# A hybrid decoder block on one core: small fp32 matmuls packed into parts of the array, gate units opened early, and splits moved in three queues

## The chip, the cores and the metric

The kernel runs on one core of one Trainium2 chip. The metric is the device time of one execution in microseconds; of several runs the median is given. The kernel drives the engines directly: TensorE (PE, its weight loads PEld), VectorE (DVE), ScalarE (ACT), GpSimd (POOL) and SyncE (SP, which issues most loads) each run their own instruction list in order, and wait for one another by semaphores alone.

## The reference, cut to what matters

```python
h = rms_norm(x, norm_mix_pre)                      # x: 512 tokens x 2048
proj = h @ w_in + b_in                             # q, f, i, g | qk, v, o, ig, fg | gate_a, gate_b
# HGRN2: 8 heads of 128, chunks of 64 tokens
q = silu(q) * 128 ** -0.5;  f = lb + (1 - lb) * sigmoid(f);  k = 1 - f
b = cumsum(log f) in a chunk;  q_dec = q * exp(b);  k_inv = k * exp(-b);  k_end = k * exp(b_last - b)
attn = tril(q_dec @ k_inv.T)                       # 64 x 64 for each head and chunk
o = attn @ v + q_dec @ S;   S = exp(b_last) * S + k_end.T @ v
y_a = head_rms_norm(o) * silu(g)
# mLSTM: 4 heads, same chunkwise form with a matrix memory -> y_b
merged = sigmoid(gate_a) * (y_a @ w_up_a) + sigmoid(gate_b) * (y_b @ w_up_b)
x = x + rms_norm(merged @ w_out, norm_mix_post)    # "x1 rows"
h = rms_norm(x, norm_ffn_pre)
out = x + rms_norm((gelu(dwconv(h @ w_gate)) * (h @ w_up)) @ w_down, norm_ffn_post)   # 5632 hidden
```

## The kernel before, in words

All data is fp32. The big products are made from two fp32r parts each: a high part, rounded by ScalarE (`split_hi`), and the rest, by VectorE (`split_lo`). A product is hi x hi + hi x lo + lo x hi. Weights of the mixer come in units of 1 MB, two units in flight (`RING`), each with its own slot s = 0 or 1 of `raw`, `w_hi` and `w_lo`. TensorE's `cm_unit` does a unit as 16 matmuls of 128x512 with `w_hi` and `h_hi`, 16 with `w_hi` and `h_lo`, 16 with `w_lo` and `h_hi`, into bank 6 or 7; ScalarE evacuates it and counts `cm_evac`. A unit's high split waits until the unit two before it is done.

The units run in this order: I, F, Q, GA (merge gates of branch a), G, QK, V, GB (gates of b), O, then the lifting and the output projection. Each engine has the order written out by hand. The recurrences are woven into the gate units: a round of HGRN2 handles 128 tokens (two chunks) beside four GA units, a round of mLSTM 128 tokens beside four GB units, four rounds each.

A round of HGRN2 on TensorE, before: 8 transposes of k_end into `hT_` (banks 0, 1); 8 score matmuls of 128x128 for both chunks at once into `hA_` (banks 2, 3); unit 0; 16 state updates that use half the rows each (L753 for the first chunk, L755 for the second); 8 matmuls of masked scores `hg_at` with v, 128x128, into `hO_` (banks 4, 5); unit 1; 16 matmuls of q_dec with the states `sa` and `sb_`, each on half of the output partitions (L767, L769); unit 2; 8 transposes of the normalised outputs; unit 3. ScalarE copies the two diagonal 64x64 blocks of each head's scores out of PSUM into `hg_at`, whose rest GpSimd has set to zero once, and GpSimd masks the upper triangle (`affine_select`). VectorE updates the states, norms the outputs and makes decays and the next round's operands (`hg_prep_b`, `hg_prep`); ScalarE does the exponentials (`hg_prep`).

The entry to the feed-forward stage: the output projection's last two column blocks are done in halves (`OUT_HALVES`, k = 0 to 3, four units each; `un_out(4, q)` and `un_out(5, q)` are the splits of k = 2 and 3). For each 128 tokens n, `mix_ms`, `x1_rows` and `x1_norm` (VectorE), `x1_square` (ScalarE) and a power on GpSimd make the residual rows and their norm. The feed-forward products run as a 2x2 block scheme with seven products (M1 to M7): operands are sums or differences of blocks. The rows are summed (`diff4`, `diff3`, `sum1`, ...), turned by TensorE (`turn_pieces(r)`, 14 of them; L917), copied as high parts (`pieces_hi`), less their high part (`less_hi`, L926), and copied as rests (`pieces_rest`); `TURN_AFTER` and `need` say which rest has to be copied before which turn or product. The weight side is `weight_sum` (VectorE), `hi` (ScalarE) and `lo` (VectorE) for each position of the sequence; `times_h` multiplies (L960 for the high part, L964 for the rest).

## Time and profile before

| | |
|---|---|
| time, median of 3 runs | 2825.56 us (2824.33 to 2825.88) |
| the profiled execution | 2820.7 us |
| its span | 2819.1 us |
| TensorE busy | 2778.4 us (99%) |
| VectorE, ScalarE, GpSimd busy | 1669.9, 1230.6, 353.5 us |
| mean granted TensorE clock | 0.998 of full speed |

Times in the profile are microseconds from the span's start. A row of the timeline merges like instructions that follow each other; a bracket gives the idle time of the engine before it and who ended it. Matmuls overlap in the pipeline, so the step from one start to the next tells the cost of one, not its duration. An fp32 matmul (not fp32r) has two records.

### The profile page before, as it was taken

The numbers are of one execution on the slowest core, as the hardware profiler recorded it, in microseconds if no ns is written. First come the engines' busy times: TensorE is split into PE (matmuls) and PEld (weight loads), VectorE is DVE, ScalarE is ACT, GpSimd is POOL, SyncE is SP. The second block draws the span as 40 slices with busy tenths as digits, with TensorE's granted clock in tenths as the row PEclk, the third lists the DMA queues.
The fourth block names the chain that finished last, engine by engine and source line by source line (L and its number), as shares of the span: only waits on it lengthen the run. The fifth ranks groups of instructions, "written<-read, shape, count | busy, mean of one in ns | idle before, by whom it ended". The sixth has DMA issues, their size and how long they took to land.

```text
span 2819.1 us, 37731 instructions
## 1 busy us (share of the span) xinstructions
PE 2778.4 (99%) x13843; PEld 2345.9 (83%) x13843; DVE 1669.9 (59%) x1863; ACT 1230.6 (44%) x1469; POOL 353.5 (13%) x417
## 2 busy tenths in 40 slices
PE   8999999999999999999989999999999999999998
PEld 6888888888888888888867888888888888888887
DVE  5232334344333323442568788888878878878788
ACT  4243444332222222222465555555555555555554
POOL 1000001000000000000000122222222222222213
PEclk9999999999999999999999999999999999999999
DMA  4333333332233334444643788888888888788876
GB/s 174 90 89 104 97 101 99 99 108 94 90 94 91 97 105 138 140 142 141 215 136 120 184 175 162 181 177 161 175 180 164 169 185 164 165 189 165 161 179 239
DMA packets 451444, 404.46 MB, mean 143 GB/s; under 512 B 13074, under 2 KB 357270, under 8 KB 448552
## 3 DMA queue, kind: packets, MB, share of 16 engines
q1 hardware_dynamic: 397672, 294.69, 34.5%
q0 software_dynamic: 49088, 100.33, 21.5%
q10 hardware_dynamic: 4608, 8.39, 0.8%
q8 instruction: 52, 0.85, 0.1%
q14 instruction: 24, 0.20, 0.0%
HBM read 302.69 MB, written 100.66 MB: 143 GB/s over the span
## 4 chain that ended last, share of the span: by engine, by line
PE 96%; DVE 2%; issue 1%; ACT 1%; POOL 0%; DMA 0%; DVEq 0%; SPq 0%; POOLq 0%; ACTq 0%
PE ps L960 19%; PE ps L615 18%; PE ps L964 10%; PE ps L618 9%; PE ps L872 6%; PE ps L997 5%; PE ps L998 5%; PE ps L999 5%; PE ps L639 4%; PE ps L641 4%; PE ps L640 4%; PE ps L677 1%; PE ps L717 0%; PE ps L1063 0%; PE ps L1059 0%
## 5 line engine op out<-in xcount | busy, mean ns | idle before, releaser
L1707 DVE TENSOR_TENSOR w_lo<-raw,w_hi 128x2048 fp32r<-128x2048 f32 x127 | 291.1, 2292 | 494.2 <-ACT w_hi L1104 494.0
L1663 POOL DMA_DIRECT2D down_sums<-arena x304 | 262.8, 972 | 904.6 <-ACT arena L1419 880.3
L1104 ACT CAST w_hi<-raw 128x2048 fp32r<-128x2048 f32 x127 | 242.2, 1907 | 237.7 <-PE ps L641 175.4
L2117 DVE TENSOR_TENSOR sum_ring<-quads 128x1024 f32<-128x1024 f32 x166 | 203.4, 1225 | 171.1 <-PE ps L964 137.4
L1375 ACT CAST op_ring<-sum_ring 128x1024 fp32r<-128x1024 f32 x166 | 175.0, 1054 | 271.2 <-DVE sum_ring L2117 271.2
L615 PE MATMUL ps<-h_hi,w_hi 128*128 128x512 f32 x1152 | 276.4, 392 | 1.1 <-ACT w_hi L1104 1.1
L618 PE MATMUL ps<-h_hi,w_lo 128*128 128x512 f32 x1152 | 272.8, 389 | 0.0
L615 PE MATMUL ps<-h_lo,w_hi 128*128 128x512 f32 x1152 | 272.8, 389 | 0.0
L960 PE MATMUL ps<-hl,op_ring 128*128 128x512 f32 x1064 | 267.5, 394 | 3.6 <-ACT op_ring L1375 2.5
L615 PEld LDWEIGHTS ps<-h_lo,w_hi 128*128 128x128 f32 x1152 | 216.2, 188 | 44.9
L618 PEld LDWEIGHTS ps<-h_hi,w_lo 128*128 128x128 f32 x1152 | 216.2, 188 | 44.9
L615 PEld LDWEIGHTS ps<-h_hi,w_hi 128*128 128x128 f32 x1152 | 214.1, 188 | 46.3 <-ACT w_hi L1104 1.5
L960 PEld LDWEIGHTS ps<-hl,op_ring 128*128 128x128 f32 x1064 | 194.3, 190 | 40.4 <-issue 2.9
L2131 DVE TENSOR_TENSOR op_ring<-sum_ring,op_ring 128x1024 fp32r<-128x1024 f32 x166 | 202.1, 1217 | 8.7 <-ACT op_ring L1375 8.7
L1419 ACT COPY arena<-ps 128x512 f32<-128x512 f32 x320 | 178.3, 582 | 53.7 <-PE ps L999 42.7
L960 PE MATMUL ps<-h,op_ring 128*128 128x512 f32 x792 | 199.4, 394 | 1.9 <-ACT h L1355 1.3
L997 PE MATMUL ps<-op_ring,act_hi 128*128 128x512 f32 x480 | 187.6, 391 | 0.1
L998 PE MATMUL ps<-op_ring,act_hi 128*128 128x512 f32 x480 | 187.5, 391 | 0.0
L999 PE MATMUL ps<-op_ring,act_lo 128*128 128x512 f32 x480 | 186.7, 389 | 0.0
L960 PEld LDWEIGHTS ps<-h,op_ring 128*128 128x128 f32 x792 | 145.1, 190 | 30.2 <-ACT h L1355 2.2
L2131 DVE TENSOR_TENSOR op_ring<-quads,op_ring 128x1024 fp32r<-128x1024 f32 x129 | 157.0, 1217 | 7.6 <-ACT op_ring L1375 7.6
L964 PEld LDWEIGHTS ps<-hl,op_ring 128*128 128x128 f32 x1064 | 145.2, 190 | 10.4
(355 smaller groups left out, 4627.2 us busy)
## 6 DMA issues: line engine op xcount, KB each, us to landing
raw<-in_w_in SPq DMA_DIRECT2D x88, 1024.0 KB, 5.3
down_sums<-arena POOLq DMA_DIRECT2D x320, 256.0 KB, 6.6
quads<-in_ffn_w_gate SPq DMA_DIRECT2D x88, 512.0 KB, 4.8
quads<-in_ffn_w_up SPq DMA_DIRECT2D x88, 512.0 KB, 4.7
quads<-in_ffn_w_down SPq DMA_DIRECT2D x88, 512.0 KB, 7.6
raw<-in_w_out SPq DMA_DIRECT2D x24, 1024.0 KB, 5.0
merge_gates<-arena ACTq DMA_DIRECT2D x32, 256.0 KB, 2.0
raw<-in_w_up_a SPq DMA_DIRECT2D x8, 1024.0 KB, 5.1
```

The source lines that it names most:

```text
L615: pe.matmul(ps[:, 6 + s, :], w[0][:, j, :], k[:, j, :], start=(k is k_hi and j == 0), stop=False)
L618: last = pe.matmul(ps[:, 6 + s, :], w[1][:, j, :], k_hi[:, j, :], start=False, stop=(j == KT - 1))
L960: pe.matmul(ps[:, bank, :], w[0][:, j, :], h[:, j, :, :].rearrange("p r t -> p (r t)"), start=(j == 0 and q not in (M7, M6)), stop=False, ...
L964: mm = pe.matmul(ps[:, bank, 0:TH], w[1][:, j, :], h[:, j, 0, :], start=False, stop=(j == HALF - 1), skip_group_check=True)
L997: pe.matmul(ps[:, n, :], act_hi[:, f + j, tok], w[0][:, j, :], start=(j == 0), stop=False)
L998: pe.matmul(ps[:, n, :], act_hi[:, f + j, tok], w[1][:, j, :], start=False, stop=False)
L999: mm = pe.matmul(ps[:, n, :], act_lo[:, f + j, tok], w[0][:, j, :], start=False, stop=(j == 1))
L1104: act.copy(w_hi[:, s, :], raw[:, s, :]).then_inc(hi_ready, 1)
L1663: pool.dma_start(dst, src, accum_op=ALU.add).then_inc(acc_added[s], 16)
L1707: dve.tensor_tensor(w_lo[:, s, :], raw[:, s, :], f32(w_hi[:, s, :]), ALU.subtract).then_inc(lo_ready, 1)
L2117: dve.tensor_tensor(op_sum[slot_of(i, pos)], quads[:, a, :], quads[:, b, :], ALU.subtract if q in (M7, M6) else ALU.add).then_inc(ff_sum, 1)
L2131: dve.tensor_tensor(op_lo[slot], src, f32(op_hi[slot]), ALU.subtract).then_inc(ff_lo, 1)
```

## The change

- **Packing.** `hg_blocks` holds the scores as 128 x 8 x 64: rows are the key tokens of both chunks, columns the 64 query tokens of the same chunk, with nothing off the diagonal. The scores are 16 matmuls (each head and chunk) with 64 columns, on the half of the output partitions that belongs to the chunk. Scores times v are 16 matmuls of 64 rows and 64 output partitions: rows by chunk, output partitions by whether the head is even or odd, bank by chunk. q_dec times state goes to the same places (`by_state`); the first chunk's part now follows directly behind scores times v, the second's comes after unit 1. ScalarE's two copies of scores are one, GpSimd's mask is two smaller ones and its zeroing is gone; the outputs' last copy is two.
- **Unit 0 of each round opens early** (`unit_opens`, `unit_goes_on`): its first 16 products stand ahead of transposes and scores, in both recurrences.
- **Queues.** ScalarE: the split of Q1 ahead of the first exponentials; in a round, the outputs' copy and squares ahead of the split of unit 3. VectorE: the outputs' norm ahead of the split and of the next round's scans. At the entry to the feed-forward stage: splits ahead of squares and of x1 rows; `x1_norm` cut into `x1_ms` and `x1_scale`; `hi(0, 1)`, `hi(0, 5)` and the copy of M1 ahead of pieces and squares; the weight sums at other places. The sum for position (0, 1) has its own room (`early_sum`), and the wait for the slot moves from VectorE to ScalarE.

```diff
--- before
+++ after
@@ -191,6 +191,8 @@
+        hg_blocks = hg_at[:, 0:HG_H * CHUNK].rearrange("p (h c) -> p h c", h=HG_H)
+        CHUNK_ROWS = (slice(0, CHUNK), slice(CHUNK, P))
@@ -247,6 +249,7 @@
+        early_sum = ar(88.5, Q)
@@ -407,6 +410,13 @@
+        def ahead(i, pos):
+            return isinstance(i, int) and (i, pos) == (0, 1)
+        def sum_of(i, pos):
+            return early_sum if ahead(i, pos) else op_sum[slot_of(i, pos)]
@@ -618,6 +628,24 @@
+            def unit_opens(u, n, s):
+                pe.wait_ge(cm_evac, n + 1)
+                w = w_hi[:, s, :].rearrange("p (j n) -> p j n", j=KT)
+                split_ready(u, 0)
+                for j in range(KT):
+                    pe.matmul(ps[:, 6 + s, :], w[:, j, :], h_hi[:, j, :], start=(j == 0), stop=False)
+            def unit_goes_on(u, n, s):
+                w = [t[:, s, :].rearrange("p (j n) -> p j n", j=KT) for t in (w_hi, w_lo)]
+                for j in range(KT):
+                    pe.matmul(ps[:, 6 + s, :], w[0][:, j, :], h_lo[:, j, :], start=False, stop=False)
+                split_ready(u, 1)
+                for j in range(KT):
+                    last = pe.matmul(ps[:, 6 + s, :], w[1][:, j, :], h_hi[:, j, :], start=False, stop=(j == KT - 1))
+                last.then_inc(unit_done, 1)
@@ -734,43 +762,54 @@
-            at_, ket, sa, sb_, on = map(heads, (hg_at, hg_ket, hg_sa, hg_sb, hg_on))
+            ket, sa, sb_, on = map(heads, (hg_ket, hg_sa, hg_sb, hg_on))
+            at_ = hg_blocks
...
+                unit_opens(U_GA + 4 * i, N_GA + 4 * i, 0)
...
-                    mm = pe.matmul(hA_[:, h, :], ki[:, h, :], qd[:, h, :], start=True, stop=True)
+                    for c, rows in enumerate(CHUNK_ROWS):
+                        mm = pe.matmul(hA_[rows, h, 0:CHUNK], ki[:, h, rows], qd[:, h, rows], start=True, stop=True)
...
-                unit(0)
+                unit_goes_on(U_GA + 4 * i, N_GA + 4 * i, 0)
...
-                pe.wait_ge(hg_scores_copied, 2 * i + 2)
+                pe.wait_ge(hg_scores_copied, i + 1)
...
-                    m1 = pe.matmul(hA_[:, h, :], ket[CHUNK:P, h, :], v_hg[CHUNK:P, i:i + 1, h * P:(h + 1) * P],
-                                   start=True, stop=True)
+                    pe.matmul(hA_[:, h, :], ket[CHUNK:P, h, :], v_hg[CHUNK:P, i:i + 1, h * P:(h + 1) * P],
+                              start=True, stop=True)
...
-                pe.wait_ge(hg_scores_masked, i + 1)
+                pe.wait_ge(hg_scores_masked, 2 * i + 2)
...
-                for h in range(HG_H):
-                    pe.matmul(hO_[:, h, :], at_[:, h, :], v_hg[:, ds(i, 1), h * P:(h + 1) * P],
-                              start=(h % 4 == 0), stop=False, skip_group_check=True)
+                for pair in range(HG_H // 2):
+                    for odd, out in enumerate(CHUNK_ROWS):
+                        h = 2 * pair + odd
+                        for c, rows in enumerate(CHUNK_ROWS):
+                            pe.matmul(hO_[out, 4 * c + pair, :], at_[rows, h, :], v_hg[rows, i:i + 1, h * P:(h + 1) * P],
+                                      start=(pair == 0), stop=False, skip_group_check=True)
+                def by_state(c, state):
+                    for pair in range(HG_H // 2):
+                        for odd, out in enumerate(CHUNK_ROWS):
+                            h = 2 * pair + odd
+                            mm = pe.matmul(hO_[out, 4 * c + pair, :], qd[:, h, CHUNK_ROWS[c]], state[:, h, :], start=False,
+                                           stop=True, skip_group_check=True)
+                    return mm
+                by_state(0, sa).then_inc(hg_update1, 1)
...
-                for h in range(HG_H):
-                    m0 = pe.matmul(hO_[0:CHUNK, h, :], qd[:, h, 0:CHUNK], sa[:, h, :], start=False, stop=False,
-                                   skip_group_check=True)
-                    m1 = pe.matmul(hO_[CHUNK:P, h, :], qd[:, h, CHUNK:P], sb_[:, h, :], start=False, stop=True,
-                                   skip_group_check=True)
-                m0.then_inc(hg_update1, 1)
-                m1.then_inc(hg_out_done, 1)
+                by_state(1, sb_).then_inc(hg_out_done, 1)
@@ -802,8 +841,6 @@
-            pe.wait_ge(tok_evac, 4 + 16)
@@ -811,6 +848,9 @@
+                unit_opens(U_GB + 4 * i, N_GB + 4 * i, 0)
+                if i == 0:
+                    pe.wait_ge(tok_evac, 4 + 16)
@@ -824,7 +864,7 @@
-                unit(0)
+                unit_goes_on(U_GB + 4 * i, N_GB + 4 * i, 0)
@@ -1187,33 +1227,44 @@
+            un_q, to_q = units_of(U_Q, 2), into(q_all, ACT.Silu, 0)
+            split_hi(*un_q(0, 1))
...
-            columns(U_Q, NU_Q, into(q_all, ACT.Silu, 0))
+            act.wait_ge(unit_done, U_Q + 1 + RING)
+            to_q(0, ps[:, 6, :], 0)
+            split_hi(*un_q(0, 2))
+            act.wait_ge(unit_done, U_Q + 1 + 1 + RING)
+            to_q(1, ps[:, 7, :], 1)
+            with act.Fori(1, NU_Q // 2) as i:
+                for s in range(2):
+                    split_hi(*un_q(i, s + 1))
+                    act.wait_ge(unit_done, U_Q + 2 * i + s + 1 + RING)
+                    to_q(2 * i + s, ps[:, 6 + s, :], s)
...
-                act.wait_ge(mem_zero, 2)
...
-                for a in (0, CHUNK):
-                    act.copy(heads(hg_at)[a:a + CHUNK, :, a:a + CHUNK], hA_[a:a + CHUNK, :, a:a + CHUNK]).then_inc(hg_scores_copied, 1)
+                act.copy(hg_blocks, hA_[:, :, 0:CHUNK]).then_inc(hg_scores_copied, 1)
...
-                split_hi(*un_ga(i, 3))
...
+                split_hi(*un_ga(i, 3))
...
-                act.copy(q_all[:, :, ds(i * P, P)], hT_).then_inc(hg_out_kept, 1)
+                act.copy(q_all[:, :, ds(i * P, CHUNK)], hT_[:, 0:4, :].rearrange("p g (e t) -> p (g e) t", e=2))
+                act.copy(q_all[:, :, ds(i * P + CHUNK, CHUNK)],
+                         hT_[:, 4:8, :].rearrange("p g (e t) -> p (g e) t", e=2)).then_inc(hg_out_kept, 1)
@@ -1315,6 +1366,8 @@
+                if k == 2 and s == 0:
+                    act.wait_ge(sq_done, 1 + TT + 2)
@@ -1371,7 +1424,9 @@
-                    src = op_sum[slot]
+                    if ahead(i, pos):
+                        slot_free(act, i, pos)
+                    src = sum_of(i, pos)
@@ -1450,10 +1505,10 @@
+            split_hi(*un_out(4, 2))
...
-            split_hi(*un_out(4, 2))
+            split_hi(*un_out(4, 3))
...
-            split_hi(*un_out(4, 3))
@@ -1469,9 +1524,9 @@
+            hi(0, 1)
...
-            hi(0, 1)
@@ -1491,9 +1546,9 @@
-            pieces_rest(10)
...
+            pieces_rest(10)
@@ -1591,14 +1646,13 @@
-            pool.wait_ge(tok_evac, 4 + 8)
-            pool.memset(hg_at, 0.0).then_inc(mem_zero, 1)
...
-                pool.wait_ge(hg_scores_copied, 2 * i + 2)
-                pool.affine_select(out=heads(hg_at), in_=heads(hg_at), compare_op=ALU.is_ge, fill=0.0, base=0,
-                                   pattern=[[0, HG_H], [1, P]], channel_multiplier=-1).then_inc(hg_scores_masked, 1)
+                pool.wait_ge(hg_scores_copied, i + 1)
+                for rows in CHUNK_ROWS:
+                    pool.affine_select(out=hg_blocks[rows, :, :], in_=hg_blocks[rows, :, :], compare_op=ALU.is_ge, fill=0.0,
+                                       base=0, pattern=[[0, HG_H], [1, CHUNK]],
+                                       channel_multiplier=-1).then_inc(hg_scores_masked, 1)
@@ -1878,16 +1932,16 @@
-                split_lo(*un_ga(i, 3))
...
-                if not last:
-                    hg_prep_b(i + 1)
+                split_lo(*un_ga(i, 3))
...
+                if not last:
+                    hg_prep_b(i + 1)
@@ -2100,9 +2154,15 @@
+            def x1_ms(n):
+                row_ms(TT + n, ss2[:, n:n + 1], 4 + n)
+            def x1_scale(n):
+                row_scale(TT + n, x1[:, n, :], g_pre2, x_rows[:, n, :], 4 + n)
...
-                row_ms(TT + n, ss2[:, n:n + 1], 4 + n)
-                row_scale(TT + n, x1[:, n, :], g_pre2, x_rows[:, n, :], 4 + n)
+                x1_ms(n)
+                x1_scale(n)
@@ -2113,8 +2173,9 @@
-                slot_free(dve, i, pos)
-                dve.tensor_tensor(op_sum[slot_of(i, pos)], quads[:, a, :], quads[:, b, :],
+                if not ahead(i, pos):
+                    slot_free(dve, i, pos)
+                dve.tensor_tensor(sum_of(i, pos), quads[:, a, :], quads[:, b, :],
@@ -2126,7 +2187,7 @@
-                    src = op_sum[slot]
+                    src = sum_of(i, pos)
@@ -2252,14 +2313,14 @@
+            split_lo(*un_out(4, 1))
...
-            split_lo(*un_out(4, 1))
+            split_lo(*un_out(4, 2))
...
-            split_lo(*un_out(4, 2))
+            split_lo(*un_out(4, 3))
...
-            split_lo(*un_out(4, 3))
+            split_lo(*un_out(4, 4))
...
-            split_lo(*un_out(4, 4))
@@ -2269,32 +2330,34 @@
+            weight_sum(0, 1)
...
-            weight_sum(0, 1)
+            lo(0, 1)
+            x1_ms(2)
...
-            lo(0, 1)
-            x1_norm(2)
-            x1_norm(3)
-            weight_sum(0, 2)
+            x1_scale(2)
+            x1_ms(3)
+            x1_scale(3)
...
-            lo(0, 2)
+            weight_sum(0, 2)
...
+            lo(0, 2)
...
-            lo(0, 4)
...
+            lo(0, 4)
```

## Rows read from the trace of the kernel before

**Rows 1.** Busy time, share and instructions of each engine (the page).
```profile
PE 2778.4 (99%) x13843; PEld 2345.9 (83%) x13843; DVE 1669.9 (59%) x1863; ACT 1230.6 (44%) x1469; POOL 353.5 (13%) x417
```

**Rows 2.** Timeline of TensorE: start, duration, engine, line, operation, count, [idle before, releaser].
```profile
210.17 3.94 PE L615 MATMUL ps<-h_hi,w_hi 128*128 128x512 f32 x16 [1.12 <-ACT w_hi L1104]
...
288.21 1.07 PE L744 MATMUL ps<-ident,arena 128*128 128x128 f32 x8 [1.56 <-issue]
...
771.53 1.16 PE L817 MATMUL ps<-arena 128*128 128x128 f32 x8 [0.79 <-DVE arena L1802]
...
1389.99 0.47 PE L639 MATMUL ps<-w_hi,hl 128*128 128x512 f32 x1 [0.90 <-DVE w_lo L1707]
```

**Rows 3.** Timeline of ScalarE around the start and the end of the Q units.
```profile
198.41 0.69 ACT L1165 ACTIVATE arena<-ps,prm 128x512 f32 x1 [7.12 <-PE ps L618]
...
208.21 1.90 ACT L1104 CAST w_hi<-raw 128x2048 fp32r<-128x2048 f32 x1
...
277.78 1.90 ACT L1104 CAST w_hi<-raw 128x2048 fp32r<-128x2048 f32 x1
```

**Rows 4.** Timeline of TensorE, first HGRN2 round.
```profile
289.11 1.95 PE L747 MATMUL ps<-arena 128*128 128x128 f32 x16
290.82 3.92 PE L615 MATMUL ps<-h_hi,w_hi 128*128 128x512 f32 x16
294.57 3.79 PE L615 MATMUL ps<-h_lo,w_hi 128*128 128x512 f32 x16
298.20 3.79 PE L618 MATMUL ps<-h_hi,w_lo 128*128 128x512 f32 x16
301.92 0.37 PE L753 MATMUL ps<-arena 64*128 64x128 f32 x1
...
302.13 0.27 PE L753 MATMUL ps<-arena 64*128 64x128 f32 x1
302.14 0.27 PE L755 MATMUL ps<-arena 64*128 64x128 f32 x1
302.24 0.27 PE L753 MATMUL ps<-arena 64*128 64x128 f32 x1
...
303.90 2.05 PE L761 MATMUL ps<-arena 128*128 128x128 f32 x16
305.71 3.90 PE L615 MATMUL ps<-h_hi,w_hi 128*128 128x512 f32 x16
...
316.95 0.27 PE L767 MATMUL ps<-arena 128*64 128x128 f32 x1
316.96 0.27 PE L769 MATMUL ps<-arena 128*64 128x128 f32 x1
```

**Rows 5.** Timeline of VectorE, first HGRN2 round.
```profile
328.28 1.22 DVE L1889 TENSOR_TENSOR arena<-arena,small 128x1024 f32<-128x1024 f32 x1
```

**Rows 6.** One line's instructions: durations in ns min/median/max, first and last start.
```profile
L800 PE MATMUL ps<-ident,arena x12: 197/198/220, 737.0 to 737.7; 4*128 4x4 f32 x12
```

**Rows 7.** Timeline of TensorE, entry to the feed-forward stage.
```profile
1439.08 1.19 PE L960 MATMUL ps<-hl,op_ring 128*128 128x512 f32 x2 [2.50 <-ACT op_ring L1375]
...
1451.35 1.09 PE L917 MATMUL ps<-ident,arena 128*128 128x128 f32 x8 [0.26 <-ACT hl L1355]
...
1471.06 1.94 PE L917 MATMUL ps<-ident,arena 128*128 128x128 f32 x16 [2.58 <-issue]
...
1475.06 2.12 PE L960 MATMUL ps<-h,op_ring 128*128 128x512 f32 x8 [0.19 <-ACT h L1355]
```

**Rows 8.** Timelines of ScalarE and VectorE, same stretch.
```profile
1470.37 0.59 ACT L1385 COPY arena<-ps 128x512 f32<-128x512 f32 x1
...
1444.83 2.35 DVE L1727 SCALAR_TENSOR_TENSOR arena<-arena,small 128x2048 f32<-128x2048 f32 x1 [0.67 <-POOL small L1574]
```

**Rows 9.** Stretches: busy of each engine, then TensorE's granted clock, DMA share, GB/s.
```profile
1439.00:1442.50 3.50, 3.42 (x8) 2.73 (x9) 2.84 (x4) 2.50 (x3) 0.55 (x1) 0.52 0.53 225
1507.00:1510.20 3.20, 3.20 (x9) 2.51 (x10) 3.17 (x5) 0.00 (x0) 0.00 (x0) 0.53 0.06 22
```

## Prediction

> **What bounds the kernel now.** I read the page first: TensorE is busy for 2778.4 of 2819.1 us [rows 1]. Work of the other engines therefore costs nothing unless TensorE stands still for it, and a change can gain in two ways only: by taking away TensorE's idle time (2819.1 - 2778.4 = 40.7 us) or by making its own instructions cheaper. So I listed TensorE's rows in order of time, for those that carry an idle time in brackets. After the first 25 us four are left ahead of the feed-forward stage [rows 2]; then come some 16 us of them between 1439 and 1516, of which [rows 7] has the turning points. From 1521 to the end there is none: what is gained earlier should reach the end.
>
> **The Q phase.** At 210.17 TensorE waited 1.12 us for a weight split on ScalarE. ScalarE's rows show why: it evacuated the last F unit at 198.41, then did the table loads and exponentials of `hg_prep(0)`, and reached the split at 208.21 [rows 3]. The change puts the split first; it can run from 199.1 to 201.0, and the exponentials end 1.9 us later, about 208.8, before unit Q0 ends (209.05). The first group behind the wait also started up slowly (3.94 us against the 3.79 of a group in mid-stream [rows 2, 4]): 1.12 + 0.15 = **1.27 us**.
>
> **The gate units opened early.** `unit_opens` puts 16 of a unit's 48 products ahead of transposes and scores. They need only the high split of that weight, which ScalarE made a unit earlier (the row at 277.78 for the unit that now starts at 286.65 [rows 3]). 16 products are 3.63 us (294.57 to 298.20 [rows 4]), so the wait for the last q times decay disappears: **1.56 us**. The same happens at the first mLSTM round: **0.79 us** [rows 2]. No product is added. What follows is 3.6 us later: the scores leave ScalarE (copies 1.2 + 1.0 us), GpSimd (one mask of 1.6 to 2.1 us, now two smaller ones, at most 4.2) and must be back when the remaining 32 products (7.26 us) are through. That is 1.0 + 4.2 = 5.2 us for the mask, plus k_end beside it: it fits, by some 2 us. In mLSTM rounds the scores were ready about 4 us after they left TensorE; 7.26 covers that too. If that cover were gone, each round would pay the excess.
>
> **DVE's new order in a round.** The normalised rows were ready at 329.50 [rows 5]; TensorE came to them with two units, three breaks and the scores behind it at 329.7: only 0.2 us to spare. Now the scans of `hg_prep_b` come behind the normalisation, ScalarE's copy of the outputs comes ahead of its split, and the second state update no longer waits for unit 1. I get the rows 2 to 3 us before TensorE wants them, and the next round's `hg_prepared` about 2 us early. Gain nil, but the tight place gets looser.
>
> **The packed small matmuls.** In fp32 each matmul is two records. A full 128x128 one with 128 columns takes 0.107 us a record (16 in 1.71 us, 289.11 to 290.82). Two that use half the rows each start within 0.01 us and a pair takes 0.11 us (302.13 to 302.24): this array does run two halves at once [rows 4]. Entering such a mode costs: the first pair came 0.09 late and the second 0.21 after it, some 0.2 us.
> - Scores, each round: from 16 records in 1.71 us [rows 4] to 16 pairs with 64 columns, two column halves. Bounds: 0.055 a pair if half the columns is half the time, 0.111 if something else sets the pace: 0.9 to 1.8 us, plus 0.2. The nearest row for very short matmuls is the 4-column transpose, a weight load and a matmul every 0.064 us (11 steps in 0.7 us) [rows 6]. I take 16 x 0.064 + 0.2 = 1.2: gain 0.5.
> - Scores times v: from 16 records in 1.81 us (303.90 to 305.71) to 32 records on quarters of the array. Four at once: 8 x 0.111 = 0.89; two at once: 1.78; one by one: 32 x 0.107 = 3.42; each plus 0.2. No row shows quarters. Rows show halves of rows sharing the array, and halves of columns (L767 and L769, 0.01 apart), each with its own moving data, and the two row halves here write different banks (4 and 5) as L753/L755 did. I take four: 1.1, gain 0.7.
> - q times state: the same 16 pairs, but half of them now directly behind the quarters: one more change of mode, loss 0.2.
>
> That is 1.0 us a round, **4.0 us** for four; bounds per round: 1.71 + 1.81 - 1.1 - 1.1 - 0.2 = +1.1 at best, 1.71 + 1.81 - 2.0 - 2.0 - 0.2 = -0.7 with only two at once and no shorter scores, -2.3 with quarters one by one. [...]
>
> **From the output projection into the feed-forward stage.** Here I followed the three queues, each row with its duration, in the new order.
> - `split_lo` of unit (4,1) stood behind the 2.35 us of `x1_rows(0)` and released TensorE at 1389.99 [rows 2]. It now starts when the high part is there (1386.2): TensorE goes on at 1389.1, 0.9 us earlier. Some comes back: x1_norm(1) now ends about 1407.6, two evacuations follow, and split (5,1) ends about 1411.05 where the unit wants it at 1410.9. Net 0.7.
> - The second product waited 2.50 us for its high part, behind `x1_square(2)` and `pieces_rest(3)` on ScalarE [rows 7]. `hi(0,1)` now goes first, but `pieces_rest(3)` still stands behind the square: start about 1437.55 instead of 1439.08, lead 1.5.
> - Turns 4 and 5 waited for x1_norm(2) and (3), whose last scale ran from 1444.83 to 1447.18 [rows 8]. With `x1_ms(2)` ahead of `x1_rows(3)` and weight sums moved back, it ends about 1444.5. Then `weight_sum(0,2)` stands behind diff3 and makes `hi(0,2)` about 1 us late relative to that: turn 7 at 1449.95 instead of 1451.35. Lead 1.4.
> - Turns 11 and 12 waited 2.58 us for M1's copy, which stood behind `pieces_rest(10)` and `hi(0,5)` at 1470.37 [rows 7, 8]. Now both come before that piece, during M1: turn 11 about 1467.35, turn 12 about 1468.35, M7 at 1471.4 instead of 1475.06. Lead **3.6 us**, the sum of this part. The later waits (1505 to 1516) hang on DVE and loads that start with it, so they move along.
>
> [...]
>
> **Sum.** 1.27 + 1.56 + 0.79 + 4.0 + 3.6 = 11.2 us, off the profiled execution's 2820.7 (span 2819.1 and 1.6 around it): 2809.5. The median of the runs lies 4.9 above the profiled one, so **2814.4 us**.
>
> **Rivals.**
> - *The packing gives nothing* because instructions, not columns, set the pace: two loads and two matmuls take 0.111 us at 128 columns, 0.028 each; 64 instructions of scores at that pace are 1.8 us, and so are those of the quarters. With the mode changes this lies between 0 and -0.7 a round. The 0.064 us for a load and a matmul is for it, the 0.01 us between two starts against it. Taken at nil: 2825.6 - 7.2 = 2818.4; chance 0.24. [...]
> - *The hand order of the feed-forward entry gives back what it gains*: split (5,1) and `weight_sum(0,2)` later than I think, lead 1 instead of 3.6: 2817.0; chance 0.12.
> - *A low clock less*: the gaps fall so that the stretch at 1507 is spared: 2814.4 - 1.5 = 2812.9; chance 0.10.
> - *Slower*: quarters of the array don't share it, nor do the 64-column pairs. Scores 32 x 0.107 = 3.4 and values 3.4 against 3.5 together is 3.3 + 0.6 a round, 15.6 in all, less 7.2 of gained waits: 2834. It decides from 1.8 us a round upwards. The pairs in step in [rows 4] speak against it; chance 0.05.
> - The forecast: 0.49.
>
> **Range and chances.** A measurement here tells about 0.2% (5.6 us) from no change, so faster means under 2819.9. Forecast, lower clock, and nearly all of the first two rivals lie below: faster 0.78. Packing at its lower bound (-0.7 x 4 = -2.8 with 7.2 gained: 2821) or both small rivals together give the same: 0.17. Slower 0.05. The lower end takes the scores at their best and the second clock drop spared, with 1 us more in the last part: 2811; the upper end takes the packing's two-at-once bound: 2821.
>
> **What would show it.** Right: no idle time at the first rows of the Q1 unit, the first transposes and the first mLSTM scores; starts of the value products in fours, a step about 0.11; the scores' 32 records in about 1.2 us; M7's first product some 3.6 us earlier relative to the start of the last output block. Wrong: the value products in 1.8 us or more; new waits of TensorE on GpSimd's mask or ScalarE's k_end copy behind the 32 products; turn 7 waiting longer than before for `pieces_rest(5)`.

## The result, and the profile after

| | before | changed |
|---|---|---|
| median of 6 runs each, alternating on one chip | 2824.94 us (2821.59 to 2826.19) | 2809.26 us (2808.70 to 2810.61) |
| the profiled execution | 2820.7 us | 2809.31 us |
| its span | 2819.1 us | 2807.5 us |

The ratio is 0.995, with a 95% interval of 0.9941 to 0.996: 15.7 us faster. The forecast was 2814.4 with a range of 2811 to 2821, so the direction was right and the time lies 1.7 us below the range. Between the two profiled executions the gain is 2820.7 - 2809.31 = 11.4 us, where the sum said 11.2. The 4.9 us that the prediction then added, from the profiled execution to the median, are not there in the changed kernel: its profiled execution and its median agree within 0.1 us. Most of what follows is about these 4.9 us.

The page of the changed kernel, first the engines:

```profile
PE 2772.3 (99%) x13971; PEld 2338.6 (83%) x13971; DVE 1671.2 (60%) x1863; ACT 1219.1 (43%) x1462; POOL 349.0 (12%) x420
```

TensorE has 128 records more than in [rows 1] and is busy for 6.1 us less. The span fell by 11.6, so 5.5 us of its idle time went too.

TensorE's timeline of the changed kernel in the first HGRN2 round (start, duration, engine, line, operation, count; L637 is the opened unit, L774 the transposes, L779 the scores, L643/L646 the rest of the unit, L798 scores times v, L805 q_dec times state):

```profile
208.76 3.79 PE L625 MATMUL ps<-h_hi,w_hi 128*128 128x512 f32 x16
...
283.79 1.30 PE L628 MATMUL ps<-h_hi,w_lo 128*128 128x512 f32 x5
284.93 3.80 PE L637 MATMUL ps<-h_hi,w_hi 128*128 128x512 f32 x16
288.56 1.04 PE L774 MATMUL ps<-ident,arena 128*128 128x128 f32 x8
289.53 1.15 PE L779 MATMUL ps<-arena 128*64 128x64 f32 x32
290.61 3.94 PE L643 MATMUL ps<-h_lo,w_hi 128*128 128x512 f32 x16
...
300.10 1.10 PE L798 MATMUL ps<-arena 64*64 64x128 f32 x32
301.13 1.09 PE L805 MATMUL ps<-arena 128*64 128x128 f32 x16
```

No row has a bracket: the waits of [rows 2] at 210.17 and 288.21 are gone. From start to start, the 32 score records take 290.61 - 289.53 = 1.08 us (1.71 before, [rows 4]; 1.2 expected), and the 32 records of scores times v 301.13 - 300.10 = 1.03 us (1.81 before, [rows 4]; 1.1 expected).

The same view at the entry to the feed-forward stage (L1000 the products, L957 the turns):

```profile
1428.72 2.12 PE L1000 MATMUL ps<-hl,op_ring 128*128 128x512 f32 x8 [1.60 <-ACT hl L1408]
...
1432.78 1.06 PE L957 MATMUL ps<-ident,arena 128*128 128x128 f32 x8 [1.00 <-DVE arena L1781]
...
1441.29 1.09 PE L957 MATMUL ps<-ident,arena 128*128 128x128 f32 x8 [1.66 <-ACT hl L1408]
...
1458.66 1.96 PE L957 MATMUL ps<-ident,arena 128*128 128x128 f32 x16 [0.26 <-issue]
...
1462.67 2.11 PE L1000 MATMUL ps<-h,op_ring 128*128 128x512 f32 x8 [0.19 <-ACT h L1408]
...
1469.54 2.96 PE L1000 MATMUL ps<-h,op_ring 128*128 128x512 f32 x8 [1.10 <-ACT h L1408]
...
1474.00 1.98 PE L1000 MATMUL ps<-h,op 128*128 128x512 f32 x8
...
1495.22 2.11 PE L1000 MATMUL ps<-h,op_ring 128*128 128x512 f32 x8 [0.56 <-DVE arena L2205]
...
1499.75 2.11 PE L1000 MATMUL ps<-hl,op 128*128 128x512 f32 x8 [1.46 <-DVE arena L2221]
```

The waits of [rows 7] have shrunk from 2.50 to 1.60 (second product) and from 2.58 to 0.26 (turn 11), while turn 7 now waits 1.66 instead of 0.26. M7's first product starts at 1462.67, 12.39 us earlier than in [rows 7]. The lead ahead of the entry is that of the last product before the wait at 1389.99 [rows 2], first before, then changed:

```profile
1388.70 0.39 PE L641 MATMUL ps<-w_hi,hl 128*128 128x512 f32 x1
```
```profile
1380.16 0.39 PE L669 MATMUL ps<-w_hi,hl 128*128 128x512 f32 x1
```

That is 8.54 us, so the entry gave 12.39 - 8.54 = 3.85 up to M7.

The granted clock of the changed kernel (stretch, its length, busy of the engines; the number after POOL is the clock):

```profile
1470.50:1473.90 3.40, 3.40 (x14) 2.96 (x13) 3.37 (x5) 1.70 (x2) 0.00 (x0) 0.51 0.00 0
```

Before, half the clock was granted at 1439 and at 1507 (0.52 and 0.53 over those stretches [rows 9]). Now there is one such stretch, at 1470.5 (0.51), behind two waits of 1.10 us for ScalarE, the later of them the bracket at 1469.54.

### The profile page after: what moved, and what is told of

It reads as the page before. It is cut to its first block, busy times and chain, and to the rows that moved or that the text cites. A ratio compares the mean times of both kernels' runs of the same rounds, so it can differ in the third digit from the quotient of the medians.

```text
span 2807.5 us, 37978 instructions
## 1 busy us (share of the span) xinstructions
PE 2772.3 (99%) x13971; PEld 2338.6 (83%) x13971; DVE 1671.2 (60%) x1863; ACT 1219.1 (43%) x1462; POOL 349.0 (12%) x420
## 4 chain that ended last, share of the span: by engine, by line
PE 96%; DVE 2%; issue 1%; ACT 1%; POOL 0%; DMA 0%; DVEq 0%; SPq 0%; POOLq 0%; ACTq 0%
PE ps L1000 20%; PE ps L625 17%; PE ps L1004 10%; PE ps L628 8%; PE ps L912 6%; PE ps L1037 5%; PE ps L1038 5%; PE ps L1039 5%; PE ps L667 4%; PE ps L669 4%; PE ps L668 4%; PE ps L643 1%; PE ps L637 1%; PE ps L646 1%; PE ps L705 1%
## 5 line engine op out<-in xcount | busy, mean ns | idle before, releaser
L2178 DVE TENSOR_TENSOR sum_ring<-quads 128x1024 f32<-128x1024 f32 x165 | 202.2, 1226 | 171.2 <-PE ps L1004 137.3
L1430 ACT CAST op_ring<-sum_ring 128x1024 fp32r<-128x1024 f32 x165 | 173.9, 1054 | 272.1 <-DVE sum_ring L2178 272.1
L1000 PE MATMUL ps<-hl,op_ring 128*128 128x512 f32 x1064 | 266.1, 392 | 2.7 <-ACT hl L1408 1.6
L625 PE MATMUL ps<-h_hi,w_hi 128*128 128x512 f32 x1024 | 245.1, 392 | 0.0
L628 PE MATMUL ps<-h_hi,w_lo 128*128 128x512 f32 x1024 | 242.5, 389 | 0.0
L625 PE MATMUL ps<-h_lo,w_hi 128*128 128x512 f32 x1024 | 242.5, 389 | 0.0
L1000 PEld LDWEIGHTS ps<-hl,op_ring 128*128 128x128 f32 x1064 | 193.2, 189 | 39.2 <-ACT hl L1408 2.0
L625 PEld LDWEIGHTS ps<-h_lo,w_hi 128*128 128x128 f32 x1024 | 192.2, 188 | 39.9
L628 PEld LDWEIGHTS ps<-h_hi,w_lo 128*128 128x128 f32 x1024 | 192.2, 188 | 39.9
L625 PEld LDWEIGHTS ps<-h_hi,w_hi 128*128 128x128 f32 x1024 | 190.7, 188 | 40.5 <-issue 0.7
L2192 DVE TENSOR_TENSOR op_ring<-sum_ring,op_ring 128x1024 fp32r<-128x1024 f32 x165 | 201.1, 1219 | 6.4 <-ACT op_ring L1430 6.4
L1000 PE MATMUL ps<-h,op_ring 128*128 128x512 f32 x792 | 198.8, 393 | 1.8 <-ACT h L1408 1.3
L1000 PEld LDWEIGHTS ps<-h,op_ring 128*128 128x128 f32 x792 | 144.6, 189 | 30.1 <-ACT h L1408 2.2
L2192 DVE TENSOR_TENSOR op_ring<-quads,op_ring 128x1024 fp32r<-128x1024 f32 x129 | 157.2, 1219 | 2.6 <-ACT op_ring L1430 2.6
```

The lines of the kernel that those rows point to most:

```text
L625: pe.matmul(ps[:, 6 + s, :], w[0][:, j, :], k[:, j, :], start=(k is k_hi and j == 0), stop=False)
L628: last = pe.matmul(ps[:, 6 + s, :], w[1][:, j, :], k_hi[:, j, :], start=False, stop=(j == KT - 1))
L1000: pe.matmul(ps[:, bank, :], w[0][:, j, :], h[:, j, :, :].rearrange("p r t -> p (r t)"), start=(j == 0 and q not in (M7, M6)), stop=False, ...
L2178: dve.tensor_tensor(sum_of(i, pos), quads[:, a, :], quads[:, b, :], ALU.subtract if q in (M7, M6) else ALU.add).then_inc(ff_sum, 1)
L2192: dve.tensor_tensor(op_lo[slot], src, f32(op_hi[slot]), ALU.subtract).then_inc(ff_lo, 1)
```

## The experiments

Each is compared with the kernel before on its own chip; a difference between two experiments is one of medians unless it says otherwise. First the kernel before itself, then the parts of the change added and undone one by one.

**e1: the kernel before, unchanged.** It tells what a comparison is worth, and shows an execution of the usual length.

> The kernel before, unchanged: its profiled execution took 2820.7 us, its timed ones mostly 2824 to 2826. Theory A (place): the 4 us sit in one stage, the entry to the feed-forward stage, where TensorE stands still and its clock falls; another profiled execution that takes 2824 or more shows them there, as one more or one longer stretch of low clock or wait. Rival B (spread): they are spread over the span, as a few ns on each transfer or matmul, or lie in the first 25 us. Ratio 1.000 either way.

Median 2824.59 us of 11 (2820.54 to 2826.12) against 2823.52 of 25, ratio 1.0002 (0.9993 to 1.0011). The profiled execution took 2825.17. Over the 89 executions of the kernel before that have their mean granted clock on record (these 11 and the 78 that ran beside the experiments), the time goes with it:

| mean granted clock | executions | time |
|---|---|---|
| 0.998, 0.999 | 35 | 2820.5 to 2821.6 us |
| 0.997 | 20 | median 2823.8 |
| 0.996 | 30 | median 2824.7 |
| 0.995 | 4 | 2825.9 to 2826.6 |

So the execution profiled before the prediction (2820.7, clock 0.998) belongs to a shorter kind, some 4 in 10. TensorE's timeline of e1, an execution of the longer kind, and its granted clock:

```profile
1439.16 2.08 PE L960 MATMUL ps<-hl,op_ring 128*128 128x512 f32 x8 [2.50 <-ACT op_ring L1375]
...
1444.32 1.71 PE L917 MATMUL ps<-ident,arena 128*128 128x128 f32 x8 [1.95 <-DVE arena L1727]
...
1455.14 2.10 PE L960 MATMUL ps<-hl,op_ring 128*128 128x512 f32 x8
...
1489.94 2.00 PE L960 MATMUL ps<-h,op 128*128 128x512 f32 x8
...
1511.32 2.12 PE L960 MATMUL ps<-h,op_ring 128*128 128x512 f32 x8 [0.56 <-DVE arena L2144]
...
1515.85 2.11 PE L960 MATMUL ps<-hl,op 128*128 128x512 f32 x8 [1.46 <-DVE arena L2160]
```
```profile
1439.10:1442.50 3.40, 3.21 (x16) 2.44 (x16) 2.74 (x4) 2.42 (x3) 0.55 (x1) 1.00 0.54 229
1444.60:1454.80 10.20, 8.00 (x33) 6.60 (x32) 8.47 (x7) 5.67 (x6) 0.32 (x2) 0.50 0.00 0
1475.30:1478.70 3.40, 3.26 (x11) 1.93 (x10) 2.58 (x4) 2.79 (x3) 0.00 (x0) 0.50 0.00 0
1485.50:1488.90 3.40, 3.40 (x8) 2.72 (x9) 2.47 (x4) 1.99 (x3) 0.00 (x0) 0.51 0.00 0
```

And the rows of the shorter execution of the same kernel, profiled before the prediction:

```profile
1444.24 1.07 PE L917 MATMUL ps<-ident,arena 128*128 128x128 f32 x8 [0.63 <-DVE arena L1727]
...
1452.20 2.10 PE L960 MATMUL ps<-hl,op_ring 128*128 128x512 f32 x8
...
1484.85 2.00 PE L960 MATMUL ps<-h,op 128*128 128x512 f32 x8
...
1506.86 3.52 PE L960 MATMUL ps<-h,op_ring 128*128 128x512 f32 x8 [0.56 <-DVE arena L2144]
...
1511.38 2.11 PE L960 MATMUL ps<-hl,op 128*128 128x512 f32 x8
```

In the shorter execution half the clock falls on the second product at 1439 [rows 9], which takes 3.58 us instead of 2.08; TensorE then waits 0.63 us for the norm rows instead of 1.95, so the slow product costs nothing. In the longer one it comes when the turns run, and stays for 10.2 us: the product behind turn 7 starts at 1455.14 instead of 1452.20, 2.9 us late. By 1489.94 against 1484.85 it is 5.1 late, after two more such stretches. Then 0.6 comes back in a wait for VectorE (the product at 1511.32 is 4.5 behind the one at 1506.86). From 1507 on the shorter execution has its own half clock, and it costs nothing: to the next product it needs 1511.38 - 1506.86 = 4.52 us, e1 at the full clock 4.53 (1511.32 to 1515.85), and the changed kernel 4.53 as well. At full clock the product ends early and waits 1.46 for VectorE; at half it fills that wait.

**e2 and e3: the entry order alone, and all but it.** e2 is the kernel before with the queues' new orders of the entry (all hunks behind `early_sum`, `ahead`, `x1_ms`/`x1_scale`, the moved splits, `hi` and copies); e3 is the changed kernel with exactly these undone.

> The kernel before with the entry part of the change alone (splits, squares, pieces and weight sums from the last half blocks on). From the two profiles this part is worth 3.0 us. Theory A: the typical execution's extra 4 us lie in that stage and go with it: about 2818 us and little spread. Rival B: about 2822 with the spread of before.

2817.21 us (2816.82 to 2818.11, 11 runs) against 2823.52: ratio 0.998 (0.9971 to 0.9989). 6.3 us faster, not 3 to 4; by its profiled execution (2817.57) it is 3.1 faster than the profiled one of before. And the spread of 5.6 us has shrunk to 1.3, with every mean clock at 0.998 or 0.999. Its profile has half the clock on the second product, as the shorter kind of before, and turn 4 then waits for nothing:

```profile
1437.44 3.47 PE L968 MATMUL ps<-hl,op_ring 128*128 128x512 f32 x8 [1.79 <-ACT hl L1365]
...
1441.91 1.04 PE L925 MATMUL ps<-ident,arena 128*128 128x128 f32 x8
```

> The changed kernel with the entry part alone taken back (packing, early openings, Q split and the order in a round stay). By the profiles 8.6 us of gain are left. Theory A: the extra time of before comes back with the old entry: 2809.3 + 3.0 + 4 = 2816 us with spread. Rival B, that the extra went with the mixer's gaps (0.8 to 1.6 us each): about 2812.3.

2815.52 us (2812.77 to 2816.48, 9 runs), ratio 0.9972. The rest is worth 8.0 us (predicted 11.2 - 3.6 = 7.6), the entry again 6.3, and the spread is back (3.7 us). The profile (2814.51) has TensorE waiting 2.50 us and 1.96 us as before, and the clock at half from 1435.6 to 1442.4, 6.8 us among the turns.

**e4: all but the packing.** Scores, mask, values and states as in the kernel before (of the diff the scores' line), early openings and queues as changed.

```diff
-                    for c, rows in enumerate(CHUNK_ROWS):
-                        mm = pe.matmul(hA_[rows, h, 0:CHUNK], ki[:, h, rows], qd[:, h, rows], start=True, stop=True)
+                    mm = pe.matmul(hA_[:, h, :], ki[:, h, :], qd[:, h, :], start=True, stop=True)
```

> The changed kernel with 128x128 scores and values again, both state products behind unit 1 (early openings and the rest stay). My sum has packing at 4.0 us: 2813.3. The profile of the changed kernel gives 16 pairs of 64-column scores 1.08 us a round and values 1.03 against 1.71 and 1.81, so 1.4 less about 0.3 for modes: 2813.7. If time that packing frees were lost again to waits behind it, 2811 or less.

2813.32 us (2813.12 to 2813.82, 5 runs), ratio 0.9965: the packing is worth 4.06 us, 1.0 a round, as predicted (4.0).

**e5: `hi(0, 1)` back behind x1_square(2) and pieces_rest(3).** One line moved on ScalarE; the wait ahead of the second product is 2.50 us again.

```diff
-            hi(0, 1)
             x1_square(2)
             pieces_rest(3)
+            hi(0, 1)
```

> The changed kernel with hi(0, 1) behind x1_square(2) and pieces_rest(3) again. By the queues the second product starts 1 us later (gap of TensorE 1.6 to 2.7 us), but turn 4 behind it waits for the norm's rows anyway: at most 0.2 us, 2809.5. If it was this gap of 2.5 us that brought the long low-clock stretches of before, they are back in most executions: about 2812 with a spread of 4 us.

2813.62 us (2811.80 to 2817.21, 5 runs) against 2824.17, ratio 0.9964 (0.995 to 0.9978): +4.4 us, where I expected 0.2 or, with the long stretches, 2.7. The profile (2814.17, 4.9 above the changed kernel's) has the wait and what follows it, in TensorE's timeline and in the granted clock:

```profile
1429.49 2.90 PE L1000 MATMUL ps<-hl,op_ring 128*128 128x512 f32 x8 [2.50 <-ACT op_ring L1430]
...
1435.87 1.06 PE L957 MATMUL ps<-ident,arena 128*128 128x128 f32 x8 [1.80 <-DVE arena L1781]
...
1446.35 2.63 PE L1000 MATMUL ps<-hl,op_ring 128*128 128x512 f32 x8
```
```profile
1430.50:1433.90 3.40, 3.40 (x13) 2.91 (x11) 2.96 (x4) 0.94 (x1) 2.59 (x1) 0.50 0.07 31
1437.30:1447.50 10.20, 8.37 (x31) 7.09 (x32) 8.40 (x7) 6.45 (x7) 0.00 (x0) 0.50 0.00 0
```

The same 10.2 us at half the clock (0.50) as in e1, among the same turns. But most of the loss is there before it: turn 4 starts at 1435.87 instead of 1432.78, 3.1 us late. VectorE shows why, first in the changed kernel, then in e5 (L2192 is `lo(0, 1)`):

```profile
1426.37 1.22 DVE L2192 TENSOR_TENSOR op_ring<-arena,op_ring 128x1024 fp32r<-128x1024 f32 x1
```
```profile
1429.38 1.23 DVE L2192 TENSOR_TENSOR op_ring<-arena,op_ring 128x1024 fp32r<-128x1024 f32 x1 [3.06 <-ACT op_ring L1430]
```

In the new order `lo(0, 1)` stands ahead of `x1_ms(2)` and `x1_rows(3)` and needs the result of `hi(0, 1)`. With `hi(0, 1)` late on ScalarE, VectorE stands still for 3.06 us and the norm rows come that much later. So 3.1 of the profile's 4.9 are a wait in a queue, and the other 1.8 come with the half clock. The two executions at a mean clock of 0.998 say the same: 2811.80 and 2812.03, 2.5 and 2.8 above the changed kernel's median.

**e6: the order of the norm rows back** (`x1_rows(3)` and `lo(0, 1)` ahead of `x1_norm(2)`). **e7: M1's copy back** behind `pieces_rest(10)`. One move each:

```diff
-            lo(0, 1)
-            x1_ms(2)
             x1_rows(3)
-            x1_scale(2)
-            x1_ms(3)
-            x1_scale(3)
+            lo(0, 1)
+            x1_norm(2)
+            x1_norm(3)
```
```diff
+            pieces_rest(10)
             hi(0, 5)
             keep_product(0, 0, M1, 3)
-            pieces_rest(10)
```

> The changed kernel with VectorE's old order at the norm (x1_rows(3), lo(0,1), x1_norm(2), x1_norm(3)). By the queues the last scale ends 2.0 us later and turn 5 with it: 2811.3, little spread. If the late turns and not the gap ahead of the second product bring the long low-clock stretch (TensorE has only short turns to do from there on), it comes back: 2814 and a spread of 4 us.

2810.47 us (2809.90 to 2811.71, 5 runs), +1.2. TensorE waits 1.96 us ahead of turn 4 again, and turn 4 is 0.9 us later. The long stretch at half clock is not in the profile, which is of the shortest execution; two of the five lie at 2811.5 and 2811.7 with a clock of 0.997, so it may be in those.

> The changed kernel with pieces_rest(10) ahead of hi(0, 5) and the copy of M1 again. By the queues turns 11 and 12 wait 2.3 us longer: 2811.6. The place lies behind the low-clock stretch of before, so no spread: if there is one, the clock hangs on the whole stage and not on its start.

2811.96 us (2810.79 to 2812.87, 5 runs), +2.7: turn 11's [2.58] is back. Here the profile has half the clock for 3.4 us among turns 4 and 5, and it costs nothing: turn 7 waits 0.70 us instead of 1.66, and the product behind it starts at 1442.10, as in the changed kernel (1442.14).

**e8: `weight_sum(0, 2)` ahead of diff3.** In the changed kernel turn 7 waits 1.66 us because `hi(0, 2)` stands ahead of `pieces_rest(5)` on ScalarE and waits for this sum. The timelines of the changed kernel, VectorE and ScalarE (L2347 is diff3, L2178 the sum, L1430 `hi`):

```profile
1435.75 2.36 DVE L2347 TENSOR_TENSOR arena<-arena 128x1024 f32<-128x1024 f32 x2
1438.03 1.22 DVE L2178 TENSOR_TENSOR sum_ring<-quads 128x1024 f32<-128x1024 f32 x1
```
```profile
1439.28 1.04 ACT L1430 CAST op_ring<-sum_ring 128x1024 fp32r<-128x1024 f32 x1 [1.30 <-DVE sum_ring L2178]
```
```diff
+            weight_sum(0, 2)
             dve.wait_ge(xn_ready, 2 + TT + 4)
...
-            weight_sum(0, 2)
+            lo(0, 2)
             for n in range(2):
                 dve.tensor_tensor(sum1[:, n, :], x_rows[:, n, LEFT], x_rows[:, 2 + n, RIGHT], ALU.add).then_inc(h_sum, 1)
-            lo(0, 2)
```

> The changed kernel with weight_sum(0, 2) ahead of the two diff3 sums and lo(0, 2) ahead of sum1, as the kernel before had them. hi(0, 2) then no longer waits 1.3 us and pieces_rest(5), turn 7 and all behind come 1.2 us earlier: 2808.1. If turn 7 then waits for diff3 instead, or the loads set the pace at the next pair, nothing: 2809.3.

2807.54 us (2806.99 to 2807.81, 5 runs) against 2824.17, ratio 0.9942 (0.9928 to 0.9956): 1.7 us faster than the changed kernel. The wait ahead of turn 7 and the clock where the changed kernel had its half stretch:

```profile
1440.28 1.09 PE L957 MATMUL ps<-ident,arena 128*128 128x128 f32 x8 [0.25 <-ACT hl L1408]
```
```profile
1470.00:1474.00 4.00, 4.00 (x26) 3.55 (x25) 3.96 (x6) 2.13 (x3) 0.00 (x0) 1.00 0.02 4
```

The 1.7 us are not the wait alone. Turn 7 starts 1.0 us earlier than in the changed kernel (1440.28 against 1441.29), the spared half clock adds 1.5 (1471.44 against 1474.00 for the same product, 2.56 in all), and 0.8 goes to a longer wait for VectorE at 1492 (1.48 us instead of 0.71).

**e9, e12, e13, e14: which idle time brings the long stretch.** All start from the kernel before. e9 puts only `hi(0, 1)` and its sum early (the gap is 1.60 us instead of 2.50). e12 is e9 with the new order of the norm rows, e13 is e9 with the new places of the splits. e14 is e2 (the whole entry) with `hi(0, 1)` back at its old place.

> The kernel before with one thing of the change: weight_sum(0, 1) early into its own room, and hi(0, 1) ahead of x1_square(2). TensorE's gap ahead of the second product falls from 2.5 to about 1.6 us; turn 4 waits for the norm's rows as before, so by the queues nothing is gained: 2824 and the spread of before. If that gap brings the long low-clock stretches, most executions lose them: a median of about 2820.8 and a spread of 1 us.

2822.70 us (2821.17 to 2823.73, 11 runs) against 2824.07, ratio 0.9997 (0.9988 to 1.0006). Missed: I had expected the long stretch to go with the gap. The profile still has one, shorter; timeline and clock:

```profile
1438.22 2.14 PE L968 MATMUL ps<-hl,op_ring 128*128 128x512 f32 x8 [1.60 <-ACT hl L1363]
...
1443.32 1.06 PE L925 MATMUL ps<-ident,arena 128*128 128x128 f32 x8 [1.95 <-DVE arena L1737]
```
```profile
1445.80:1452.60 6.80, 5.70 (x23) 4.44 (x22) 6.09 (x6) 4.18 (x5) 0.00 (x0) 0.50 0.00 0
```

> The kernel before with hi(0, 1) first and with VectorE's new order at the norm (lo(0, 1), x1_ms(2), x1_rows(3), x1_scale(2), x1_ms(3), x1_scale(3)); weight_sum(0, 2) stays ahead of diff3. By the queues turn 5 starts some 2 us earlier and so does all behind it: 2820.8 at the short low-clock stretches. If both idle times of TensorE in that stage (ahead of the second product and ahead of turn 4) together bring the long stretch, the median is 2819 to 2820 and the spread 1 us. If the place of the stage in time decides, and not its idle times, the spread of before stays and the median is 2822.

2820.50 us (2819.81 to 2822.64, 11 runs) against 2822.10, ratio 0.9992 (0.9983 to 1.0001). Eight of the eleven lie at 2819.8 to 2820.6, three at 2822.5.

> The kernel before with hi(0, 1) first and with the splits of the half blocks ahead of x1 rows and squares. By the queues the last output block starts 0.7 us earlier, and turns 4 and 5 with it: 2822.0 with the long low-clock stretches as in the kernel with hi(0, 1) first alone, 2820.1 without. If only the sum of idle times counts, they stay, since turn 4 still waits 2 us.

2821.83 us (2819.67 to 2822.54, 11 runs), ratio 0.9996 (0.9987 to 1.0005): four at 2819.7 to 2820.3, seven at 2821.8 to 2822.5. With the second idle time in place most executions still have the loss. (What the longer executions of e12 and e13 have was not profiled; both profiles are of the shorter kind.)

> The kernel before with the whole entry part but hi(0, 1) behind x1_square(2) and pieces_rest(3) again. On the changed kernel that cost 4.4 us and brought the long low-clock stretch. If the gap decides, the same here: 2821.5 and spread. If it was the place in time on the changed kernel, about 2817.4 and little spread.

2821.36 us (2820.64 to 2823.19, 11 runs), ratio 0.9998 (0.9989 to 1.0007). That is 4.1 us more than e2 for one moved line, with the spread back (2.6 us). The profiled execution (2820.64, clock 0.998) has no long stretch and is still 3.1 us longer than e2's:

```profile
1438.19 3.38 PE L968 MATMUL ps<-hl,op_ring 128*128 128x512 f32 x8 [2.50 <-ACT op_ring L1387]
...
1444.56 1.06 PE L925 MATMUL ps<-ident,arena 128*128 128x128 f32 x8 [1.78 <-DVE arena L1739]
```

Turn 4 starts 1444.56 - 1441.91 = 2.65 us later than in e2, by the same wait of VectorE for `hi(0, 1)` (3.06 us). So about 3 of the 4.1 us are the queue's, and about 1 is left for the clock.

**e10: no early openings.** Both `unit_opens` gone, `unit(0)` whole behind the scores again; new queue orders kept.

```diff
-                unit_opens(U_GA + 4 * i, N_GA + 4 * i, 0)
...
-                unit_goes_on(U_GA + 4 * i, N_GA + 4 * i, 0)
+                unit(0)
```

> The changed kernel with unit 0 of each round in one piece behind transposes and scores again. By the sum the waits at the first HGRN2 and the first mLSTM round come back, 1.56 + 0.79: 2811.6. If the 16 products also covered something in later rounds, more; if the packed round leaves the operands ready anyway, less.

2814.17 us (2813.82 to 2814.35, 7 runs), +4.9 where 2.35 was expected. TensorE's timeline shows where the rest is, at the first transposes of the second round, and the like ([0.65], [0.66]) at 392.87 and 445.92:

```profile
286.80 1.06 PE L773 MATMUL ps<-ident,arena 128*128 128x128 f32 x8 [1.56 <-issue]
...
339.82 0.44 PE L773 MATMUL ps<-ident,arena 128*128 128x128 f32 x2 [0.66 <-DVE arena L1901]
```

In the kernel before these rounds had no wait. VectorE's new order puts the scans behind the norm and makes the next round's operands 0.66 us late for transposes that come first; behind 16 products they are in time. At the turn that the changed kernel starts at 1422.84 this one is 5.5 us late (1428.37); 1.5 come back since it has no half clock at 1470, and 1.0 goes again to the wait for VectorE (1.72 us instead of 0.71).

**e11: scores times v by chunk, not by quarters.** The same 32 records, first all of chunk 0, then all of chunk 1, so that neighbours use the same half of the rows and differ in the output half alone.

```diff
-                for pair in range(HG_H // 2):
-                    for odd, out in enumerate(CHUNK_ROWS):
-                        h = 2 * pair + odd
-                        for c, rows in enumerate(CHUNK_ROWS):
+                for c, rows in enumerate(CHUNK_ROWS):
+                    for pair in range(HG_H // 2):
+                        for odd, out in enumerate(CHUNK_ROWS):
+                            h = 2 * pair + odd
```

> The changed kernel with the 16 value matmuls in another order: first all of chunk 0 (rows 0 to 63), then all of chunk 1, so that neighbours differ in output half alone. Two at once: 16 x 0.11 = 1.78 us a round instead of 1.03, 3.0 us in all: 2812.3. If what matters is only that each uses a quarter, nothing: 2809.3.

2810.61 us (2810.46 to 2811.30, 5 runs), +1.35 where 3.0 was expected. TensorE's timeline:

```profile
300.14 1.59 PE L798 MATMUL ps<-arena 64*64 64x128 f32 x32
301.67 1.09 PE L805 MATMUL ps<-arena 128*64 128x128 f32 x16
```

The step is 1.53 us instead of 1.03: four rounds make 2.0, of which 0.7 is not lost in the end: this execution has no stretch at half clock at 1470 (1.5), and its wait for VectorE is 0.7 longer (1.45 us instead of 0.71). Quarters do share the array four at a time: in windows of 0.01 us the changed kernel has 4 of these records under way at 300.11, 8 at 300.29 and 12 at 300.38, so they start in fours about 0.11 us apart. In e11 there are 2 at 300.20, 4 at 300.35 and 6 at 300.44. Of the 0.78 us that quarters save against 1.81, this order keeps 0.28.

## Why the prediction was wrong in its number and right in its sum

**The failed step** is the last of the sum: "The median of the runs lies 4.9 above the profiled one, so 2814.4". It carried over a difference as if it were a constant of the measurement. It was a cost of the kernel, in the very stretch that the change edits: some 6 of 10 executions of the kernel before are of a longer kind, and the one of them that was profiled (e1) is granted half the clock (0.50) for 10.2 us among turns 4 to 7 and for two shorter stretches after that. The new entry alone takes the longer kind away (e2), and the old entry alone brings it back (e3). The changed kernel has none among its six, so it gained the term as well: 11.4 + about 4.3.

**What brings these stretches** was narrowed down and not settled. All four profiles with 6.8 us or more at half the clock in one go have a long second idle time: TensorE waits 1.95 (e1), 1.96 (e3), 1.80 (e5) and 1.95 us (e9) ahead of turn 4. The first, ahead of the second product, is 2.50 in three of them and 1.60 in e9, so the longer gap there is not needed. Shortening it alone did not help either: 3 of 11 executions of e9 are of the shorter kind, against 35 of 89 before. With both idle times shortened (e12) it is 8 of 11, with the first and the splits instead (e13) 4 of 11; with so few executions the shares are rough. No profile in which the first is at most 1.79 and the second at most 1.04 has over 3.4 us in one go (changed kernel, e2, e4, e7, e8, e10, e11, e12). The reverse does not hold: e6, e13 (both 1.60 and 1.96) and e14 (2.50 and 1.78) have a long second idle time and no long stretch in their profiles, though each of these executions is the shortest of its run or the second shortest. In the shorter execution of before the half clock at 1439 slowed the product ahead of turn 4 and so shortened the wait there to 0.63 us; the two can't be told apart in it. So a long wait ahead of turn 4 goes with the stretches and does not always bring them; what tips a single execution was not found. e5 and e14 do not weigh the first gap by itself, since both idle times are long in them and most of their loss is VectorE's wait.

**The half clock at 1439** [rows 9] was covered by the wait for the norm rows in the profiled execution only (0.63 us left of 1.95). In a longer one it is not at 1439 but at 1444.6, among turns and copies that take turns, and no idle time shrinks by as much.

**The half clock at 1507** is 1.5 us in the rival that takes it off (3.2 x (1 - 0.53) [rows 9], an estimate). No run shows this term: from 1506.86 to the next product it takes 4.52 us with half the clock and 4.53 without (e1). The stretch at 1507 went away and gave nothing, while the new one at 1470.5 costs 1.5 at first: between M7's first product and the row at 1474.00 the lead over before falls from 12.39 to 1484.85 - 1474.00 = 10.85. Half of that comes back: the wait for VectorE behind it is 0.71 us instead of 1.48 (at 1493.44 and 1505.09). The rival that a low clock less would make it faster had the direction and neither place nor size.

**The other terms**, in the profiles:

| step | predicted | measured |
|---|---|---|
| split of Q1 | 1.27 | 1.4 |
| first HGRN2 round opened early | 1.56 | 1.6 |
| first mLSTM round opened early | 0.79 | 1.1 |
| packing, four rounds | 4.0 | 4.06 (e4) |
| entry | 3.6 | 3.85 at M7, 3.1 at 1511; by medians 6.3 (e2, e3) |

Where no experiment is named, the measured ones are leads between starts that answer to each other in the two timelines, less the lead that was there already. The small excess in the first and third has one source: an idle bracket begins where the last matmul ends, but in mid-stream the next starts some 0.16 us before that end (283.79 + 1.30 against 284.93), and the group behind a gap starts up 0.15 us slower (3.94 us against 3.79 [rows 2, 4]). A bracket of 1.12 is thus worth 1.4, and one of 0.79 is worth 1.1. The entry lost 1.5 to the clock at 1470.5 and had 0.8 given back by the wait for VectorE, hence 3.1. So the sum came out near the profile (11.2 and 11.4) partly by luck: the waits gave 0.5 more than predicted and the clock took 0.7. Its single moves are worth, undone from the whole, 4.4 (`hi(0, 1)`, of which 3.1 by way of VectorE), 1.2 (norm order; the trace's step is 0.9) and 2.7 (M1's copy; 2.3 by the wait that [rows 7] shows).

**The packing's rivals fell.** Instructions do not set the pace: 64 of them (loads and matmuls) take 1.03 us in quarters, 0.016 us each, where the rival took 0.028. The value taken for the scores, from the 4-column transposes, was 0.1 too dear. Where the 0.2 us at a change of mode comes from (the first pair 0.09 late, the second 0.21 after it [rows 4]), no run tells.

**"Gain nil" for VectorE's new order** was right only together with the early openings; alone it costs three waits of 0.66 us (e10).

**Weight sum (0, 2) "about 1 us late"** was seen, and its effect was in the sum: turn 7's lead from the entry is 1451.35 - 1441.29 - 8.54 = 1.5 where 1.4 was predicted. But it is also the wait of 1.66 that the prediction named as a sign of being wrong, and it could be had: e8 gets 1.7 us of the median back by one more move.

## What to carry to other kernels

When the profiled execution lies outside the range of the other runs, ask what the others have that it lacks, before adding the difference to a forecast; here the mean granted clock beside each time would have said it. A move is judged by all that waits for its result, not by the nearest wait: `hi(0, 1)` lengthened TensorE's own wait by 0.9 us, but held VectorE for 3.06 and turn 4 for 3.1. Only what is left after such waits (1.8 of 4.9 us in e5) is the clock's. A price for half the clock has to be taken to the next wait: if that wait shrinks by as much, it is nothing (4.52 us with half the clock, 4.53 without, at 1507). And a new order on one engine is free only with the cover that it was made for.

## What the runs showed of the hardware that was not expected

- Half the clock was granted for 10.2 us in one go (e1, e5) while TensorE was busy for 8.0 and 8.4 of them. The longest idle time of TensorE ahead of it in this stage was 2.50 us in both.
- Half the clock among the turns can be free: in e7 turn 7's wait shrank from 1.66 to 0.70 us and the next product came on time.
- Two column halves with 64 columns each run at 1.08 us for 16 pairs, 0.068 a pair, against 0.111 for a pair of row halves at 128 columns [rows 4].
- Four quarters side by side need 1.03 us for 32 records of 128 columns; the same records ordered by chunk, which at first start in twos (about 0.11 us apart from 300.30 on), need 1.53, not the 1.78 that 16 pairs of 0.111 would make. Between 300.65 and 301.18 the trace of e11 has 6 to 12 of them under way in windows of 0.01 us, where up to 300.62 it had 2 to 6, so some there overlap by more than pairs; why was not tried.
